# Residual products with the activations stationary and the weights moving, and the residual stream kept by tokens

## The reference, cut to what matters

```python
x = x + mixer(rms_norm(x, norm_mix[i]))              # two mixers (MLA, mLSTM), each ending in y @ w_o
x = x + sqrelu_mlp(rms_norm(x, norm_ffn[i]), w1, w2) # relu(h @ w1)**2 @ w2, hidden width 4096
h = h + 0.5 * swiglu_ffn(rmsnorm(h, g), w_in, w_out) # four times, hidden width 2816
h = h + short_conv_mixer(rmsnorm(h, g), ...)         # ends in (b * y) @ w_out
h = h + nsa_mixer(rmsnorm(h, g), ...)                # ends in out @ w_o
```

## Time and profile before

| | |
|---|---|
| median of 3 runs | 1685.65 us (1682.8 to 1685.79) |
| the profiled execution's own time | 1682.93 us |
| its span, first to last instruction | 1681.2 us |
| PE busy | 1622.9 us, 97% |
| DVE, ACT, POOL busy | 1099.1, 885.4, 163.5 us |
| mean granted TensorE clock | 0.985 of full |

### The profile page before, as it was taken

The page is one execution under the profiler, slowest core; times in us unless marked ns, Lnnn a source line. Parts: engine busy times, 40 slices in busy tenths (PEclk is TensorE's granted clock), DMA queues, the critical chain, the costliest instruction groups (busy, mean ns, idle before and its releaser), DMA issues.

```text
span 1681.2 us, 33598 instructions
## 1 busy us (share of the span) xinstructions
PE 1622.9 (97%) x11652; PEld 1530.4 (91%) x11652; DVE 1099.1 (65%) x1770; ACT 885.4 (53%) x1468; POOL 163.5 (10%) x141
## 2 busy tenths in 40 slices
PE   7899999999999999999999999998999988799999
PEld 7789998977999899998999999898999877799997
DVE  6667666544866666667877666785566727676665
ACT  5676554535655445445446445544645547664443
POOL 1740000266000000000000000000000053300000
PEclk9999999989999999999999999999999989999999
DMA  6136556543555656556655555656455670055554
GB/s 226 63 90 195 180 188 189 174 137 126 187 180 185 190 173 200 180 183 200 194 182 187 182 181 186 212 179 202 148 184 185 214 159 13 1 176 186 178 191 144
DMA packets 81246, 282.81 MB, mean 168 GB/s; under 512 B 8848, under 2 KB 12432, under 8 KB 81168
## 3 DMA queue, kind: packets, MB, share of 16 engines
q1 hardware_dynamic: 77376, 276.88, 51.4%
q10 hardware_dynamic: 3792, 4.85, 1.7%
HBM read 280.12 MB, written 1.57 MB: 168 GB/s over the span
## 4 chain that ended last, share of the span: by engine, by line
PE 90%; DVE 4%; ACT 3%; issue 1%; DMA 1%; ACTq 1%; POOL 0%; DVEq 0%; SPq 0%
PE psum L1651 18%; PE psum L1653 18%; PE psum L1652 18%; PE psum L1643 16%; PE psum L1644 9%; PE psum L1779 2%; PE psum L1781 2%; PE psum L1780 2%; ACT arena L853 1%; DMA raw<-tiles 1%; PE psum L2034 1%; PE psum L1941 0%; DVE arena L1517 0%; DVE arena L1516 0%; PE psum L1846 0%
## 5 line engine op out<-in xcount | busy, mean ns | idle before, releaser
L510 ACT ACTIVATE w_hi<-raw 128x1024 fp32r<-128x1024 f32 x522 | 549.8, 1055 | 474.4 <-PE psum L1653 281.1
L968 DVE TENSOR_TENSOR w_lo<-raw,w_hi 128x1024 fp32r<-128x1024 f32 x476 | 581.8, 1223 | 227.6 <-ACT w_hi L510 227.1
L1651 PE MATMUL psum<-xs,w_hi 128*128 128x256 f32 x1960 | 556.7, 284 | 5.8 <-DVE w_lo L968 4.8
L1653 PE MATMUL psum<-xs,w_lo 128*128 128x256 f32 x1960 | 555.2, 283 | 0.0
L1652 PE MATMUL psum<-xs,w_hi 128*128 128x256 f32 x1960 | 555.1, 283 | 0.0
L1643 PE MATMUL psum<-hs,w_hi 128*128 128x512 f32 x1216 | 421.8, 390 | 0.0
L1651 PEld LDWEIGHTS psum<-xs,w_hi 128*128 128x128 f32 x1960 | 376.6, 192 | 6.9 <-DVE w_lo L968 5.2
L1652 PEld LDWEIGHTS psum<-xs,w_hi 128*128 128x128 f32 x1960 | 376.7, 192 | 0.2
L1653 PEld LDWEIGHTS psum<-xs,w_lo 128*128 128x128 f32 x1960 | 376.7, 192 | 0.0
L1644 PE MATMUL psum<-hs,w_lo 128*128 128x256 f32 x1216 | 342.9, 282 | 0.0
L1643 PEld LDWEIGHTS psum<-hs,w_hi 128*128 128x128 f32 x1216 | 228.3, 188 | 47.6
(11 more groups left out here) (282 smaller groups left out, 1644.7 us busy)
## 6 DMA issues: line engine op xcount, KB each, us to landing
raw<-tiles SPq DMA_DIRECT2D x522, 512.0 KB, 4.3
bias<-bias_dram ACTq DMA_DIRECT2D x8, 256.0 KB, 12.0
x<-x_in SPq DMA_DIRECT2D x4, 256.0 KB, 5.8
y_out<-x SPq DMA_DIRECT2D x8, 128.0 KB, 3.3
con<-consts SPq DMA_DIRECT2D x1, 771.0 KB, 9.1
bias_dram<-bias_row ACTq DMA_DIRECT2D x1, 512.0 KB, 7.2
row<-rows SPq DMA_DIRECT2D x1, 192.0 KB, 8.7
vec<-vecs SPq DMA_DIRECT2D x1, 80.5 KB, 2.1
```

What stands on the lines that cost most here:

```text
L510: act.activation(w_hi[s][:, :], raw[s][:, :], ACT.Copy).then_inc(hi_ready, 1)
L968: dve.tensor_tensor(w_lo[s][:, :], raw[s][:, :], hi_of(w_hi[s][:, :]), ALU.subtract).then_inc(lo_ready, 1)
L1651: pe.matmul(out, w_hi[s][:, c:c + P], x_hi, start=first, stop=False)
L1653: return pe.matmul(out, w_lo[s][:, c:c + P], x_hi, start=False, stop=last)
```

## The change

Every residual product is turned round: 128 tokens of `x_hi` or `x_lo` are stationary and 512 weight columns move. `x` is kept by tokens (`TB` = 2 blocks of 128 tokens, each 1024 wide), the weights of these products are stored by `token_tiles`, and `out` stages shrink from 24 tiles to 22 (the old layout padded them). An output is now 128 tokens x 512 features: group g = 0, 1 of features, blocks tb = 0, 1.

```diff
-    ("up_0", 32, 32), ("down_0", 32, 8),
-    ("glu_0", 44, 44), ("out_0", 24, 8), ("cin", 24, 24), ("cout", 8, 8), ...
+    ("up_0", 32, 32), ("down_0", 32, 4),
+    ("glu_0", 44, 44), ("out_0", 22, 4), ("cin", 24, 24), ("cout", 8, 4), ...
@@ PE
-            def residual(name, per, chunks, src, ready):
-            def residual_one(name, src, ready, between=None):
+            def residual(name, chunks, src, ready, between=None):
+                def block(g, c, tb):
+                    s, col = (t0 + g * half_ + c // 2) % RING, c % 2 * 512
+                    x_hi, x_lo = (src[:, c * 2 * S + part_ * S + tb * P:][:, 0:P] for part_ in range(2))
+                    out = bank((o0 + 2 * g + tb) % 4)
+                    pe.matmul(out, x_hi, w_hi[s][:, col:col + 512], start=c == 0, stop=False)
+                    pe.matmul(out, x_hi, w_lo[s][:, col:col + 512], start=False, stop=False)
+                    return pe.matmul(out, x_lo, w_hi[s][:, col:col + 512], start=False, stop=c == chunks - 1)
...
+                            for tb in range(TB):
+                                for c in pair:
+                                    ins = block(g, c, tb)
+                                if tb == 0:
+                                    ins.then_inc(out_done, 1)
+                        ins.then_inc(tile_done, 1)
+                        if g == 1 and j == 1 and name in NEXT:
+                            turn_x(NEXT[name], 0)
+            def turn_x(norm_, half_):
+                pe.wait_ge(out_read, OUT0[RES[res]] + 2 * half_ + 2)
+                if half_:
+                    pe.wait_ge(xs_ready, XS0[norm_] + 4)
+                for k in range(4 * half_, 4 * half_ + 4):
+                    for tb in range(TB):
+                        ins = pe.transpose(x_turned(k)[:, tb * P:(tb + 1) * P], x[:, tb * D + k * P:tb * D + (k + 1) * P], ident)
+                    ins.then_inc(x_turn, 1)
@@ PE, sums: for every norm behind a residual product
-                        ins = pe.matmul(bank(RB, 0, S), ones[:, :], ssq[:, :], start=True, stop=True)
-                            ins = pe.matmul(bank(STAT, tb, tb + 1), ssq[:, tb * P:(tb + 1) * P], ones[:, 0:1], start=True, stop=True)
+                    pe.wait_ge(diag_ready, BROADCAST.index(name) + 1)
+                    pe.wait_ge(xs_ready, XS0[name] + KD)
+                    ins = pe.matmul(bank(RB, 0, S), ones[:, :], diag[:, :], start=True, stop=True)
@@ ACT, residual
+                    act.activation(sq[tb][:, :], x_cols(g, tb), ACT.Square,
+                                   accum_out=row_ssq[:, 2 * g + tb:2 * g + tb + 1]).then_inc(row_sq, 1)
+                    if norm_ and j == chunks - 1:
+                        squares(1, 0)
+                        squares(1, 1)
+                        x_hi(4)
+                        x_hi(5)
+                        act.wait_ge(row_summed, res + 1)
+                        act.activation(std[:, 0:TB], row_sum[:, :], ACT.Sqrt, bias=eps[:, 0:1], scale=1.0 / D).then_inc(std_ready, 1)
+                        x_hi(6)
+                        x_hi(7)
+                    split(t0 + j + RING)
@@ DVE, residual
+                    if j in (half_ - 1, chunks - 1):
+                        add((j + 1) // half_ - 1, 0)
+                        add((j + 1) // half_ - 1, 1)
+                    if norm_ and j == chunks - 1:
+                        x_lo(4)
+                        dve.wait_ge(row_sq, 4 * res + 4)
+                        dve.tensor_tensor(row_sum[:, :], row_ssq[:, 0:TB], row_ssq[:, TB:2 * TB], ALU.add).then_inc(row_summed, 1)
+                        x_lo(5)
+                        x_lo(6)
+                        row_factors(norm_)
+                        x_lo(7)
+                    take_lo(t0 + j + RING)
+                    if norm_ and j in (half_ + 1, half_ + 2):
+                        for k in (0, 1) if j == half_ + 1 else (2, 3):
+                            x_lo(k)
```

More of the change, by code:

```diff
@@ L53 @@
 FF2 = 2816 // P
-FF2_TILES = -(-FF2 // BLK)
 TAPS = 3
@@ L167, in build @@
         stdb = sb("stdb", [P, S])
+        diag = sb("diag", [P, S])
+        row_ssq = sb("row_ssq", [P, 2 * TB])
+        row_sum = sb("row_sum", [P, TB])
+        row_scale = sb("row_scale", [P, TB])
         rb = sb("rb", [P, S])
@@ L571, in up, with pre_1_hi @@
+            def pre_1_hi(k):
+                act.wait_ge(xs_ready, XS0["kvn"] + k + 1)
+                act.activation(hi_part(os_, k), x_turned(k), ACT.Copy, scale=vec[:, VEC["pre_1"] + k:VEC["pre_1"] + k + 1]).then_inc(pre_hi, 1)
             def up(name):
@@ L697, in mlstm @@
             def mlstm():
-                root("mix_1")
+                row_factors("mix_1")
                 used("mgate", 2)
@@ L758, in nsa_kv @@
             def nsa_kv():
-                root("kvn")
-                used("kv", 8)
-                for k in range(KD):
-                    split_x(hi_part(os_, k), x[:, k * S:(k + 1) * S], vec[:, VEC["pre_1"] + k:VEC["pre_1"] + k + 1])
+                used("kv", 2)
+                for k in range(4, KD):
+                    pre_1_hi(k)
+                used("kv", 6, 2)
+                row_factors("kvn")
+                used("kv", 8, 6)
                 act.wait_ge(out_read, OUT0["kv"] + 4)
@@ L942, in _ @@
             nsa()
-            residual_one("wo_n")
-            root("post_1")
+            residual("wo_n", KD)
+            row_factors("post_1")
             glu("glu_3")
-            residual("out_3", FF2_TILES)
+            residual("out_3", FF2)
         @block.vector
@@ L1605, in _ @@
             mla()
-            residual_one("wo_a")
-            norm("ffn_0")
+            residual("wo_a", KD)
             up("up_0")
-            residual("down_0", 4)
-            norm("mix_1")
+            residual("down_0", FF1)
             mlstm()
-            residual_one("wo_m")
-            norm("ffn_1")
+            residual("wo_m", KD)
             up("up_1")
-            residual("down_1", 4)
-            norm("pre_0")
+            residual("down_1", FF1)
             glu("glu_0")
-            residual("out_0", FF2_TILES)
-            norm("mid_0")
+            residual("out_0", FF2)
             conv()
-            residual_one("cout")
-            norm("post_0")
+            residual("cout", KD)
             glu("glu_1")
-            residual("out_1", FF2_TILES)
-            norm("kvn")
+            residual("out_1", FF2)
             nsa_kv()
             glu("glu_2", {0: keys, 4: keys_turned, 9: compression_bias, 15: compressed})
-            residual("out_2", FF2_TILES)
-            norm("mid_1")
+            residual("out_2", FF2)
             nsa()
-            residual_one("wo_n")
-            norm("post_1")
+            residual("wo_n", KD)
             glu("glu_3")
-            residual("out_3", FF2_TILES)
+            residual("out_3", FF2)
         @block.tensor
         def _(pe):
-            def product(out_bank, lhs, k, src, first, last, hi=0):
-                s, c = lhs
-                chunk = k * 2 * S
-                pe.matmul(bank(out_bank), w_hi[s][:, c:c + P], src[:, chunk:chunk + 2 * S], start=first, stop=False)
-                return pe.matmul(bank(out_bank, 0, S), w_lo[s][:, c:c + P], src[:, chunk:chunk + S], start=False, stop=last)
             def narrow_product(out_bank, lhs, k, src, first, last):
@@ L1783, in token_major @@
                         ins.then_inc(tile_done, 1)
-                    if norm_ and n == chunks // 2:
+                    if norm_ in NORMS[2:] and n == 0:
+                        turn_x(norm_, 1)
+                    if norm_ and n == (12 if norm_ == "kvn" else chunks // 2):
                         sums(norm_)
@@ L2084, in _ @@
             mla()
[L2085 removed]
+            residual("wo_a", KD, os_, after(xs_ready, XS0["o_a"]), turn_others("o_a", o_tok, (a_o, H)))
             feature("up_0", FF1, "ffn_0", norm_="ffn_0")
[L2087 removed]
+            residual("down_0", FF1, hs, after(hs_ready, hid0["up_0"]))
             mlstm()
[L2089 removed]
+            residual("wo_m", KD, os_, after(xs_ready, XS0["o_m"]),
                          {3: lambda: turn_outputs("o_m", m_h, (m_gated, 2), [4, 5, 6]),
```

388 lines of the change are left out of this document (183 added, 205 removed), and 8 rows, old and new, of the table STAGES.

## The result

The changed kernel takes **1699.89 us** (median of 4 runs, 1698.34 to 1701.61) against 1685.72 for the kernel before on the same chip (4 runs, 1682.8 to 1688.94): ratio 1.0087, 95% interval 1.0075 to 1.01. That is 14.2 us more. The forecast was 1697.5 with a range of 1688 to 1712. The profiled execution took 1698.77 us, its span is 1697.0.

The account below looks back on a forecast made before the run. TensorE was taken as the bound, through its matmul stream and its waits. Terms -5.9 - 3.6 + 15.0 - 0.7 + 4.0 + 3.0 = +11.8 us on the 1685.65 median gave 1697.5 us, range 1688 to 1712.

Parts of the forecast that it names:

- stream of `down`, `out` (152 chunks): In down and out, a chunk goes from 2.774 to 2.735 us, 0.039 less: -5.9 us over 152 chunks.
- stream of the 8-chunk products: In wo_a, wo_m, cout and wo_n, a chunk goes from 2.846 to 2.735 us: -3.6 us over 32 chunks.
- 17 bursts: Behind residual products, each burst of eight turns on TensorE costs 0.88 us with nothing hiding it: +15.0 us.
- column sums, and waits ahead of the sums that have gone: Column sums of mix_1 and kvn fall away, 0.37 us each: -0.7 us.
- seams of the four 8-chunk products: Behind wo_a, wo_m, cout and wo_n, TensorE waits 1.0 us each, 0.9 of it ahead of the turns: +4.0 us.
- entry to NSA: At ngate and nq, ScalarE issues the bias transfers later, so late weight tiles end later: +3.0 us, bounds 0 to 4.
- This last is exactly the form that the residual products get: kv's steps, activations stationary and 512 weight columns moving, give the residual products' price: 0.2279 us each.
- If the transfer starts 3.0 later: At NSA's entry, bias transfers leave at +5.6 instead of +2.6, so TensorE's next limit ends 3.0 us later.
- Long hand-offs: At the seams, engine hand-offs stay at the loop's 0.27 us: waits of 11.7 instead of 4.0, total 1705; chance 0.14.
- The clock at the seams: Clock falls to 0.50 once at each of nine seams, 1.7 us each: +15.3, total 1713; chance 0.16.
- NSA shorter: In NSA, nq's weights land ahead of the bias transfer, removing the 5.5 us wait: -12.3, total 1682; chance 0.10.

Follow-up runs that it names:

- Experiment 7: Changed kernel with an unused 128-byte tile ahead of hs, so that hs starts at a multiple of 256 bytes: 1686.36 us.
- experiment 6: Changed kernel with every burst of eight transposes at the seams issued twice: 1711.06 us.
- experiment 3: Kernel before with an unused 1120-byte tile ahead of rb, so that os and hs lie where the changed kernel has them: 1689.5 us.
- experiment 8: Changed kernel with the four DMAs of the compression's weights issued by POOL behind kvc, not by ACT: 1686.46 us.
- experiment 12: Kernel before with xs alone moved by 64 bytes; os and hs moved by 256, one full period: 1672.78 us.
- experiment 1: Changed kernel with its four new small tiles allocated last, so that os and hs lie as in the kernel before: 1701.29 us.
- experiment 5: Changed kernel plus matmuls behind its last product, varying both operands' places, some behind a small fp32 matmul or a transpose: 2096.28 us, one run.
- experiment 9: Changed kernel with xs 64 bytes past a multiple of 256, hs at a multiple, and the compression's weights issued by POOL: 1667.7 us.
- experiments 9 and 11: The second of the two: kernel before with xs and os 64 bytes past a multiple of 256, compression's weights issued by POOL: 1662.53 us.
- experiments 4: Changed kernel plus matmuls behind its last product, other engines idle, for several places of the activation operand: 1842.56 us, one run.

## Why the prediction was right, and where only its sum was

The size was forecast at +11.8 us and measured at +14.2 (+15.8 between the two profiled executions). The terms, forecast and as the traces have them:

| term | forecast | measured |
|---|---|---|
| stream of `down`, `out` (152 chunks) | -5.9 | +2.3 |
| stream of the 8-chunk products | -3.6 | -1.5 |
| 17 bursts | +15.0 | +14.9 |
| column sums, and waits ahead of the sums that have gone | -0.7 | -2.5 |
| seams of the four 8-chunk products | +4.0 | +1.8 |
| other waits in these four (`w_lo` in three of them) | none | +1.4 |
| entry to NSA | +3.0 | -2.1 |
| the rest of NSA | none | +1.6, clock |
| stall in `glu_2` | none | +2.1, of the run |
| shorter steps in `glu_2` | none | -3.6, 3.2 of it of the run |
| the rest of `glu_2` | none | -0.7 |
| ahead of `wo_a`, clock near 40 us | none | +3.1, of the run |
| mixer (-0.4), end (-0.7) | none | -1.1 |

They are read from the starts of the stages in both traces and sum to +15.7; the spans differ by 15.8. Behind `down_0`, `down_1`, `out_0` and `out_1` the next stage pays 0.87 for the burst and gets 2.5 us back in all: 0.7 are the two column sums, 0.75 the waits of 0.25 ahead of the sum, which the prediction did not count; most of the rest lies in `kv`. Behind the entry to NSA the clock was granted 0.50 for 20.5 us in the trace after and for 13.6 in the one before; for all of NSA the traces of the experiments have from 10.2 to 23.9, so this too I count to the run.

**The stream** is a step that failed, though the total did not show it. "A chunk of `down` or `out` [...] will cost 12 x 0.2279 = 2.735" took `kv`'s row, which is fed from `xs` at place 0; `hs` was to lie at 128, where a step is 232.4 ns and a chunk 2.789, more than the 2.774 of before. "This last is exactly the form that the residual products get" was right for the form and not for the place. A row with the other value stood in the trace before: `uq`, fed from `os`, ran at 233 ns. Experiment 7 puts `hs` at 0 and gets 226.7. The same for the 8-chunk products, 233.3 from `os` and 232.4 from `hs` in `cout`.

**The bursts** came out as the row had them, 0.87 each, and doubled once more 0.87 (experiment 6). This term is right by its mechanism, and it is larger than the whole. The Trainium skill's figure (TensorE: Matmul & The Clock Gate, Part 4: PE-mode transpose), about 275 ns for a transpose, is no distance between starts here: a turn takes 0.11 us of TensorE.

**The seams.** Long products wait for nothing, as laid out. The short ones wait 0.39 and not 0.9 ahead of the turns, and nothing further on: the additions ended at +1.8 and not at +2.3 (behind `wo_a` they run from 138.41 to 139.69, the product ends at 137.93). Nothing was tried on it, since it is worth 2 us.

**The entry to NSA** had the wrong sign. "If the transfer starts 3.0 later" failed first: ACT issues it 3.1 us behind the end of `out_2` (1357.69 - 1354.60), not 5.6; the issues go out while the copies that stand ahead of them in the program still run (the last begins at 1358.10). Before it was 2.6. The last late weight tile then lies with ACT at +25.0 (1379.57) and not at +27.0. Why it comes 2 us earlier was not tried. The fall of the clock to 0.50 of the earlier trace rows, 1345.6 to 1349.0, is absent in the trace after (1.00 from 1359.5 to 1377.0), but it is not the whole of it: the trace of experiment 3 has no such fall either, and its stretch from `out_2` to the attention is 30.3 us. The four traces with the old seam have 30.3 to 31.5, the nine with the new one and single bursts 28.4 to 30.0.

**The stall in glu_2** is ACT's issues, shown by experiment 8. The two large issues took 3.59 and 6.18 us in the trace after and 2.94 and 4.75 in the one before. The length changes from trace to trace and not with the kernel: 6.10, 7.06 and 6.23 us in those of the kernel before and of experiments 3 and 12, from 6.13 (experiment 1) to 8.20 in those built on the changed one with the issues left on ACT. So the 2.1 us are not the change's.

**The shorter steps in glu_2** are the change's only for the part from 118.3 to 117.8 (0.4 us), by the place of `os`; the rest, to 113.3, comes and goes with places and program the same (experiments 1 and 5).

**The start.** Between 37 and 48 us the clock was granted 0.84 in the trace before and 0.53 in the one after. Later runs of either kernel show both kinds: 0.60 in experiment 12, built on the kernel before, 0.84 in experiment 9, built on the changed one. From the first product fed from `os` to `wo_a` it takes 77.9 to 80.3 us in the four traces with the old seams and 77.9 to 80.9 in the others. So I count it to the run and not to the change.

**The rivals.** Long hand-offs: the 30 steps of chunks 2 to 6 behind each burst take 3.67 to 3.68 us where 30 x 0.120 are 3.60, so there was no wait worth the name; in `ngate` two waits of 0.4 and 0.2 came, where 0.8, 0.3, 0.4 and 0.3 were laid out. The clock at the seams: full in every window around a burst, even of sixteen. The rule of the Trainium skill (TensorE: Matmul & The Clock Gate, Part 4: PE-mode transpose) that transposes don't count as busy changed nothing at a seam here, where they make up 0.8 us between long streams. NSA shorter: 2.1 us, not 12.3; the wait of 5.5 stayed (5.47).

So the range and the side were right because the bursts were; that the errors of the other terms (8.2 and 2.1 too low, 1.8, 2.2 and 5.1 too high, and seven not seen) nearly cancel was luck. With better places for each kernel the change costs some 3 to 5 us (experiments 9 and 11): 152 chunks of 12 x 0.2268 = 2.722 save 7.9, the turns cost 14.9. No other places of `hs` were tried for the old form. From these numbers I estimate that the change would pay only where there are over 17 chunks for each burst (0.87 / 0.052), over 34 for a product with two; the longest here has 32.

## What to carry to other kernels

Before a step's price is taken from another stage, look whether it reads from another tile: two rows of the same form with different tiles (227.9 and 233) are a warning that the place counts. Where TensorE is the bound, try the offset of the activations against the weights: 64 bytes ahead of one tile were worth 12 us of 1686, nearly as much as the whole restructuring cost (14). And an engine that feeds the bound should not issue large DMAs while an idle one could: it took 10.5 us out of `glu_2` here, 8.2 of them the wait. Before a difference between two profiled executions is put down to a change, look how much the same stretch differs between other traces: the stall, the clock near 40 us, the clock in NSA and the rhythm of `glu_2` differed by 2 to 3 us each with no edit to account for it.

## What the runs showed of the hardware

A matmul's step depends on the distance in SBUF of the stationary from the moving operand, with a period of 256 bytes: 117.2 to 120.3 ns for 256 columns in 57 of the 64 groups of experiment 5, most at equal places; for 512 columns, with the activations stationary, 226.7 to 227.4 at equal places and 229 to 234 at the others. It is so with all other engines idle (experiments 4 and 5). The distance does not settle it alone: at one distance a stream of 256 columns can run in a second steady rhythm, up to 4.5 ns away. It was 113.3 for 117.8 over the last 600 steps of `glu_2` in four traces of six with the same places, in two groups of experiment 5 and behind one push; `cout` had 116.7, 117.8 and 120.0 with `hs` at one place. Behind the stall of 8.2 us in `glu_2` the clock was granted 0.50, and the next 3.35 us of matmuls ran at 1.2 GHz. The stretch behind the stall cost 2.3 us more than without it (10.5 less 8.2), most of it by that. Eight transposes of 128 x 128 in a stream cost 0.87 us and sixteen 1.75, with the clock at full around them. Four DMA issues that held ScalarE for 10.4 us took GpSimd 3.6.
